# A hybrid transformer step: four accumulation groups at once after each norm, another order of work on VectorE and ScalarE, and GpSimd's low parts in half pieces

## The chip, the cores and the metric

The kernel runs on one core of one Trainium2 chip. The metric is the device time of one execution in microseconds (us), taken as the median of three runs. All arithmetic is in float32; the large matrix products run on TensorE in the fp32r form.

## The reference, cut to what matters

The reference is one inference step of a two-layer backbone with 640 tokens (512 latent and 128 context) and 1024 features. The part that matters here is the order of the norms and the projections behind them:

```python
h = rmsnorm(x, norm_g[layer, 0]) * (1 + sc1) + sh1
if layer % 2 == 0:            # layer 0: convolution module beside 4 retention heads
    u_val, u_gate, q, k, v, g = split(h @ w_in)
    y = concatenate([conv_out, ret_out]) @ w_out
else:                         # layer 1: grouped-query attention with per-head norm and rotary positions
    q, k, v = split(h @ w_qkv)
    y = blocked_attention(apply_rope(rms(q)), apply_rope(rms(k)), v) @ w_o
x = x + g1 * y
h = rmsnorm(x, norm_g[layer, 1]) * (1 + sc2) + sh2
x = x + g2 * (square(relu(h @ mlp_w1)) @ mlp_w2)
```

The scales, shifts and gates (`sh1`, `sc1`, `g1`, ...) come from a vector product `silu(cond) @ ada_w`, of which 1024x6144 weights are read per layer.

## The kernel before, in words

**Products.** The activations lie transposed in SBUF, features on the partitions, in two halves of 320 tokens. Every factor is kept as a high part and a low part (`hH`, `hL` for activations, `wH`, `wL` for weights), and a product is three matmuls per 128-feature chunk k (high by high, high by low, low by high), added up in one PSUM bank over eight chunks. `product` (L471) writes these matmuls for one or several *groups* at once; a group is one bank, that is 128 output features by 320 tokens (or 128 tokens by 256 features). Its matmul is line 479 in the profile.

**Weight tiles.** The weights come in 96 tiles of 1024x256. A tile goes through four steps, each in two halves of 1024 columns: SP loads a half into `raw`, of which there is only one copy; ScalarE rounds it into `wH` (`split`, L983); GpSimd writes `wL = raw - wH` (`lo`, L1366), and that frees the half of `raw` for the load of the next tile. `wH` and `wL` have two slots, tile t uses slot t % 2. TensorE waits for `wl_done` of the first half at chunk 0 and of the second at chunk 4 (`w_wait`).

**Pairs of tiles behind a norm.** Behind each norm stands `tile_pair` (or `qkv_pair`): two tiles, both slots, by two halves of tokens, eight groups. Groups 0 and 1 are tile 0 on the first half of tokens, 2 and 3 tile 1 on the first half, 4 and 5 tile 0 on the second half, 6 and 7 tile 1 on the second half. They run two at a time. So slot 0 is no longer read once groups 4 and 5 are done, and the `split` of the tile after the pair is put there on ScalarE.

**The norm.** DVE (VectorE) adds the squares that ScalarE makes (`square`, `add_squares`), TensorE adds them over the partitions with a product by ones (`stat`, L601), ScalarE takes the root (`std`), DVE the reciprocal (L1409, 2.2 us), and then for each chunk DVE writes `vb` (`h_value`, L1419), ScalarE `hH` (`hi`, L1004), DVE `hL` (`h_lo`, L1429). Chunk k of a half of tokens releases `h_ready`, for which TensorE waits at chunk k. The first half of tokens (`h_both`) is interleaved with the last residual updates `xT += gate * ps` (L1387) of the product before, which also free banks 0 to 3 for the pair, and with the squares of the second half. The second `stat` stands inside the first two groups of the pair.

**The heads.** The four retention heads are projected in two passes i of six tiles b. DVE does the 31 taps of the depthwise convolution in between (`taps`, L1543), cut into pieces around the heads' work. At the end ScalarE copies the last outputs to `ret`, DVE normalises them (L1618) and multiplies by the gate (L1623), TensorE turns them in 16 pieces (`turn_retention`, L610), ScalarE copies `hH`, DVE writes `hL` (L1634). Eight of these pieces stand before the output projection, eight before its chunk 7. The convolution's channel sums (L1641 to L1649) follow on DVE.

**Attention's entry.** `qkv_pair` runs keys and first queries; then come tiles 2 to 5 (`tile_n`). DVE does head norm and rotation (`rope`, L1788 to L1808), for which ScalarE takes a root (`rope_std`, L1257); TensorE turns keys and queries (`turn_keys`, L877; `turn_queries`, L889) into banks 4 to 6, and ScalarE copies them out (`turned_out`, L1264).

**The scale vectors.** `strips` (L590) multiplies 512x512 pieces of `ada_w`, which SP loads into the single buffer `ada` once the piece before is used. On SP the third piece stands behind the load of weight tile 3, because `load_ada(t)` follows `load_tile(t + 1, ...)`.

Of the kernel before, what the change touches and what calls it, by code (L numbers as in the profile page):

```python
# [71 lines left out]
N_TILES = T_MLP1 + 8 * FG  # L72

# [33 lines left out]
QKV_PAIR = ((0, 0), (0, 1), (1, 0), (1, 1), (0, 2), (0, 3), (0, 4), (1, 2), (1, 3), (1, 4))  # L107
# [66 lines left out]
def hybrid_step(nc, x_prompt, x_sample, state_ret, cache_k, cache_v, ada_w, even_w_in, even_w_out, final_g,  # L174
# [3 lines left out]
    with ctx:  # L178
# [73 lines left out]
        fr = place("fr", [P, 2, HALF])  # L252
# [48 lines left out]
        wh_done, wl_done = sem("wh_done"), sem("wl_done")  # L301
# [38 lines left out]

        block = ctx.enter_context(nc.Block())
# [3 lines left out]
        def _(sp):  # L345
# [4 lines left out]
            def load_tile(t, halves, first=False):  # L350

                for j, src in enumerate(halves):
                    if not first:
                        sp.wait_ge(wl_done, 2 * t - 1 + j)
                    n = src.shape[2]
                    sp.dma_start(raw[:, j, :].rearrange("p (k n) -> p k n", n=n), src).then_inc(raw_in[j], 16)
# [113 lines left out]
        def _(pe):  # L470
            def product(groups, nk, waits, width):  # L471


                for k in range(nk):
                    waits(k)
                    for bank, lhs, rhs in groups:
# [7 lines left out]
            def w_wait(t, k, nk):  # L484

                if k == 0:
                    pe.wait_ge(wl_done, 2 * t + 1)
                elif k == nk // 2:
                    pe.wait_ge(wl_done, 2 * t + 2)

            def tile_t(t, slot, xH, xL, free, x_wait=None, hooks=None, nk=KC, nm=2, bank0=0, inside=None, pairs=False):
# [12 lines left out]
                for n in range(0, 2 * nm, together):  # L504
# [3 lines left out]
                    def waits(k, n=n):  # L508
                        if n == 0:
                            w_wait(t, k, nk)  # L510
                        if inside and inside[:2] == (n, k):
                            inside[2]()
# [7 lines left out]
            def tile_pair(t, xH, xL, free, x_wait=None, hooks=None, nk=KC, nm=2, inside=None, together=1):  # L520
# [8 lines left out]
                for n in range(0, 4 * nm, together):  # L529
                    for q in range(n, n + together):  # L530
                        free(q)
# [8 lines left out]
                    product([group(q) for q in range(n, n + together)], nk, waits, HALF)  # L540
                    for q in range(n, n + together):
# [17 lines left out]
            def qkv_pair(t, free, x_wait, inside):  # L559
# [8 lines left out]
                for ns in ((0, 1), (2, 3), (4, 5), (6,), (7, 8), (9,)):  # L568
                    for q in ns:
                        free(q)  # L570
# [8 lines left out]
                    product([group(q) for q in ns], KC, waits, 256)  # L579
# [74 lines left out]
            for j, (n0, n1) in enumerate(((6, 9), (9, 13), (13, 16), (16, 16))):  # L654
# [4 lines left out]
                for n in range(n0, n1):  # L659
# [4 lines left out]
                      {1: [lambda: strips(0)], 5: [lambda: strips(1)]}, together=2)  # L664
# [95 lines left out]
            for n in range(8):  # L760
                turn_retention(n)

# [7 lines left out]
            for t in range(4):  # L770
                def free(n, t=t):
                    if t == 0 and n < 4:
                        pe.wait_ge(act_free, A_MLP0 - 3 + n)
                    else:
# [4 lines left out]
                       inside=(0, 7, lambda: [turn_retention(n) for n in range(8, 16)]) if t == 0 else None,  # L779
# [69 lines left out]
            def mlp(layer, norm):  # L849
# [5 lines left out]
                          inside=(0, 4, lambda: stat(norm, 1, SUMS)), together=2)  # L855
# [27 lines left out]
            def turn_queries(r):  # L883
                pe.wait_ge(ro_done, 2 * r + 4)
                pe.wait_ge(tr_out, 3 * (r + 1))
                for h in range(2):
                    cs = slice(h * P, (h + 1) * P)
                    for n, tile in enumerate(LAT_TILES):
# [7 lines left out]
                     lambda half, k: pe.wait_ge(h_ready, 16 * 2 + 8 * half + k + 1), (0, 4, lambda: stat(2, 1, SUMS)))  # L896
# [75 lines left out]
        def _(act):  # L972
# [35 lines left out]
            def before_pair_ends(norm, v0, t, start):  # L1008

                std(norm, 0)  # L1010
                hi(norm, 0, range(0, 3))
                square(norm, 12, v0, "tile")
                square(norm, 13, v0, "tile")
                split(t, 0, start - 2)
                hi(norm, 0, range(3, 6))
                square(norm, 14, v0, "tile")
                square(norm, 15, v0, "tile")
                split(t + 1, 1, start)
                hi(norm, 0, range(6, 8))
# [27 lines left out]
            hi(0, 1, range(0, 4))  # L1047
# [9 lines left out]
            hi(0, 1, range(4, 8))  # L1057
# [34 lines left out]
            for i in range(2):  # L1092
                at = 0
                for b in range(6):
# [7 lines left out]
                    for n in range(4 if b < 2 else NT):  # L1102
# [15 lines left out]
                        if b in (3, 5) and n == 3:  # L1118
                            for q in range(3):
# [5 lines left out]
                                                     ACT.Copy).then_inc(o_out, 1)  # L1125
# [821 lines left out]
```

## Time and profile before

| | |
|---|---|
| time, median of 3 runs | 1694.05 us (1691.47 to 1695.34) |
| the profiled execution's own time | 1695.47 us |
| its span, first to last instruction | 1693.7 us |
| TensorE busy | 1619.5 us, 96% |
| VectorE (DVE) busy | 770.2 us, 45% |
| ScalarE (ACT) busy | 528.1 us, 31% |
| GpSimd (POOL) busy | 503.2 us, 30% |
| mean granted TensorE clock | 0.98 |

The span is almost wholly TensorE. What a change around it is worth is read from the places where TensorE stands still. The span leaves out 1.8 us that lie around it in the execution's own time.

### The profile page before, as it was taken

The page shows a single profiled execution, that of the slowest core. Times are in us where ns is not written, and L with a number is a line of the kernel's source. Part 1 is how long each engine was busy: PE and PEld are TensorE (multiplying, and loading weights), DVE is VectorE, ACT ScalarE, POOL GpSimd, SP SyncE. Part 2 cuts the span into 40 slices and gives each one's busy share as a digit, 9 for nine tenths or more (in the row PEclk, how much of TensorE's full clock was granted, in tenths as well). Part 3 has the DMA queues.
Part 4 walks back from the last instruction along what each step waited for, and adds up shares of the span by engine and source line. Part 5 has one row for each costly group of instructions (what it writes and reads, how often), then busy time and mean ns, then how long its engine had stood idle before and what let it go on. Part 6 is the DMA issues. An engine that isn't in the chain of part 4 may idle for free.

```text
span 1693.7 us, 27621 instructions
## 1 busy us (share of the span) xinstructions
PE 1619.5 (96%) x11934; PEld 1539.0 (91%) x11934; DVE 770.2 (45%) x1438; ACT 528.1 (31%) x986; POOL 503.2 (30%) x198
## 2 busy tenths in 40 slices
PE   5899998989899999999999989999999999999998
PEld 3899998979899999999999889556999999999997
DVE  4547675656662232242232865653572241331333
ACT  3413332324442132131232423543352131231332
POOL 0335234313233333333323233000233333333331
PEclk8999999999999999999999999999999999999999
DMA  8444333202243233343343122000222222222221
GB/s 298 141 158 127 117 113 125 88 26 69 87 149 125 94 132 125 125 148 105 105 142 111 57 75 69 13 1 1 79 85 75 75 76 75 75 75 75 75 75 63
DMA packets 131019, 162.16 MB, mean 96 GB/s; under 512 B 4433, under 2 KB 103633, under 8 KB 130897
## 3 DMA queue, kind: packets, MB, share of 16 engines
q1 hardware_dynamic: 129664, 159.34, 29.0%
q8 instruction: 94, 1.54, 0.4%
q10 hardware_dynamic: 1232, 1.05, 0.2%
q14 instruction: 29, 0.23, 0.0%
HBM read 156.44 MB, written 3.93 MB: 95 GB/s over the span
## 4 chain that ended last, share of the span: by engine, by line
PE 86%; DVE 8%; ACT 2%; POOL 1%; DMA 1%; issue 1%; SPq 0%; DVEq 0%; ACTq 0%
PE ps L479 74%; PE ps L590 2%; PE ps L944 2%; DVE hL L1429 2%; POOL wL L1366 1%; PE ps L909 1%; DMA pre_over_h<-in_ada_w 1%; PE ps L685 1%; DVE amx L1819 1%; PE ps L718 1%; DVE vb L1419 1%; ACT wH L983 1%; PE ps L610 1%; PE ps L923 1%; DVE xT L1387 1%
## 5 line engine op out<-in xcount | busy, mean ns | idle before, releaser
L1366 POOL TENSOR_TENSOR wL<-raw,wH 128x1024 fp32r<-128x1024 f32 x192 | 500.2, 2626 | 1158.1 <-ACT wH L983 1157.9
L479 PE MATMUL ps<-hH,wH 128*128 128x320 f32 x1536 | 482.6, 314 | 12.5 <-DVE hL L1429 7.1
L479 PE MATMUL ps<-hL,wH 128*128 128x320 f32 x1536 | 477.3, 311 | 0.0
L479 PE MATMUL ps<-hH,wL 128*128 128x320 f32 x1536 | 477.3, 311 | 0.0
L479 PE MATMUL ps<-fH,wH 128*128 128x320 f32 x1024 | 317.6, 310 | 0.0
L479 PE MATMUL ps<-fH,wL 128*128 128x320 f32 x1024 | 316.2, 309 | 0.0
L479 PE MATMUL ps<-fL,wH 128*128 128x320 f32 x1024 | 316.2, 309 | 0.0
L479 PEld LDWEIGHTS ps<-hH,wH 128*128 128x128 f32 x1536 | 291.2, 190 | 19.4 <-issue 9.5
L983 ACT ACTIVATE wH<-raw 128x1024 fp32r<-128x1024 f32 x192 | 193.0, 1051 | 346.9 <-PE ps L479 328.9
L479 PEld LDWEIGHTS ps<-hL,wH 128*128 128x128 f32 x1536 | 291.1, 190 | 0.6 <-issue 0.4
L479 PEld LDWEIGHTS ps<-hH,wL 128*128 128x128 f32 x1536 | 290.8, 189 | 0.0
L1387 DVE SCALAR_TENSOR_TENSOR xT<-ps,modT,xT 128x320 f32<-128x320 f32 (+2 forms) x264 | 107.4, 436 | 388.3 <-PE ps L479 388.2
L1735 DVE TENSOR_TENSOR fs<-fr 128x320 f32<-128x320 f32 x128 | 79.4, 621 | 265.0 <-ACT fr L1219 264.1
L479 PEld LDWEIGHTS ps<-fH,wH 128*128 128x128 f32 x1024 | 192.5, 188 | 1.7 <-issue 1.6
L479 PEld LDWEIGHTS ps<-fL,wH 128*128 128x128 f32 x1024 | 192.5, 188 | 0.1
L479 PEld LDWEIGHTS ps<-fH,wL 128*128 128x128 f32 x1024 | 192.5, 188 | 0.0
L479 PE MATMUL ps<-wH,hH 128*128 128x256 f32 x560 | 164.6, 294 | 4.8 <-POOL wL L1366 4.3
L479 PE MATMUL ps<-wL,hH 128*128 128x256 f32 x560 | 160.2, 286 | 0.0
L479 PE MATMUL ps<-wH,hL 128*128 128x256 f32 x560 | 160.2, 286 | 0.0
L1219 ACT ACTIVATE fr<-ps 128x320 f32<-128x320 f32 x128 | 55.7, 437 | 279.3 <-PE ps L479 279.2
L479 PEld LDWEIGHTS ps<-wH,hH 128*128 128x128 f32 x560 | 109.4, 195 | 6.4 <-issue 4.0
L479 PEld LDWEIGHTS ps<-wL,hH 128*128 128x128 f32 x560 | 109.4, 195 | 0.5 <-issue 0.2
(190 smaller groups left out, 1591.5 us busy)
## 6 DMA issues: line engine op xcount, KB each, us to landing
raw<-in_mlp_w SPq DMA_DIRECT2D x128, 512.0 KB, 3.9
ada<-in_ada_w SPq DMA_DIRECT2D x40, 1024.0 KB, 5.2
raw<-in_even_w_in SPq DMA_DIRECT2D x32, 512.0 KB, 5.8
raw<-in_even_w_out SPq DMA_DIRECT2D x12, 512.0 KB, 3.6
raw<-in_odd_w_qkv SPq DMA_DIRECT2D x12, 512.0 KB, 3.6
pre_over_h<-in_ada_w SPq DMA_DIRECT2D x2, 2048.0 KB, 14.9
pre_arena<-in_ada_w SPq DMA_DIRECT2D x2, 2048.0 KB, 18.7
raw<-in_odd_w_o SPq DMA_DIRECT2D x8, 512.0 KB, 3.4
```

The lines of the kernel that those rows point to most:

```text
L479: last = nc.tensor.matmul(ps[:, bank, 0:width], a_, b_, start=(k == 0 and p_ == 0), stop=(k == nk - 1 and p_ == 2))
L590: last = nc.tensor.matmul(ps[32 * j:32 * j + 32, B_ADA, 0:P], siluc[:, 4 * part + k, :], by_lane[:, j], start=(part == 0 and k == 0), stop ...
L610: return nc.tensor.transpose(ps[:, bank, at:at + np_], src[p0:p0 + np_, tile, col0:col0 + P], ident[p0:p0 + np_, p0:p0 + np_])
L685: return nc.tensor.matmul(ps[:, bank, at:at + RV], kd_nat[:, r, tile, :], v_nat[:, tile, :], start=True, stop=True)
L718: last = nc.tensor.matmul(out, qdec[:, r, cs], S[:, r, n, :], start=False, stop=(r == 1))
L944: last = nc.tensor.matmul(ps[:, 6, :], va[:, vt, kv * P:(kv + 1) * P], pT[:, h % 2, n, :], start=(n == 0), stop=(n == 4))
L983: nc.scalar.activation(wH[:, slot, j * 1024:(j + 1) * 1024], raw[:, j, :], ACT.Copy).then_inc(wh_done, 1)
L1219: nc.scalar.activation(fr[:, n % 2, :], ps[:, n % 4, 0:HALF], ACT.Relu).then_inc(act_free, 1)
L1366: nc.gpsimd.tensor_tensor(wL[:, slot, cs], raw[:, j, :], wH[:, slot, cs].bitcast(F32), ALU.subtract).then_inc(wl_done, 1)
L1387: last = nc.vector.scalar_tensor_tensor(out=x, in0=ps[:, n % 4, c0 - half * HALF:c0 - half * HALF + w_], scalar=modT[:, gate_at + k, which ...
L1429: last = nc.vector.scalar_tensor_tensor(out=hL[:, k, c0:c0 + w_], in0=vb[:, k % 4, a_:a_ + w_], scalar=modT[:, SHIFT_AT[norm] + k, which:w ...
L1735: nc.vector.tensor_tensor(fs[:, n % 2, :], fr[:, n % 2, :], fr[:, n % 2, :], ALU.mult).then_inc(fs_done, 1)
```

## The change

- **Groups of four.** In `tile_pair` and `qkv_pair` the first four groups still run two by two, but groups 4 to 7 now run together: for each chunk twelve matmuls instead of six. In `qkv_pair` the ten groups are also renumbered, and the last two run together. ScalarE's `split` of the tile after the pair moves from behind groups 4 and 5 to behind group 7 (attention: behind group 8 of 10).
- **Later sums.** The second `stat` moves from chunk 4 to chunk 6 of the first two groups.
- **VectorE and ScalarE order around the norms.** The last residual updates and squares are interleaved earlier. In the MLP `fr` has four buffers, and ScalarE does four `relu` before the larger part of the second half's `hi`. In attention, `rope_std(0)` moves behind the `split` of tile 3, `turn_keys` from inside tile 2 to behind it, `turn_queries(0)` into tile 3, and `turned_out(0)` behind `rope_std(2)`.
- **GpSimd pieces.** Every half is written by two instructions of 512 columns instead of one of 1024.
- **VectorE low parts.** The low parts of tiles `T_HEADS + 2` and `T_HEADS + 8` move from GpSimd to DVE, behind four of the taps (`weight_lo`).
- **Heads' end.** The copies of the heads' outputs and the last root move ahead of the last two gate copies; six pieces instead of eight stand before the output projection, the other ten between its chunks; the first low part stands before the last gate product.

```diff
-                for n in range(0, 4 * nm, together):
-                    for q in range(n, n + together):
-                        free(q)
+                for ns in joint or [(n,) for n in range(4 * nm)]:
+                    n = ns[0]
+                    if len(ns) < 4:
+                        for q in ns:
+                            free(q)
...
-                      {1: [lambda: strips(0)], 5: [lambda: strips(1)]}, together=2)
+                      {1: [lambda: strips(0)], 3: [lambda: strips(1)]}, joint=((0, 1), (2, 3), (4, 5, 6, 7)))
...
-                          inside=(0, 4, lambda: stat(norm, 1, SUMS)), together=2)
+                          inside=(0, 6, lambda: stat(norm, 1, SUMS)), joint=((0, 1), (2, 3), (4, 5, 6, 7)))
...
-                for ns in ((0, 1), (2, 3), (4, 5), (6,), (7, 8), (9,)):
+                for ns in ((0, 1), (2, 3), (4, 5, 6, 7), (8, 9)):
...
-            for n in range(8):
+            for n in range(6):
                 turn_retention(n)
+            TURN_AT = {(0, 4): (6, 7), (0, 5): (8,), (0, 6): (9, 10), (0, 7): (11, 12), (2, 1): (13, 14), (2, 2): (15,)}
...
             for t in range(2, 6):
                 tile_n(T_QKV + t, t % 2, lambda n, t=t: pe.wait_ge(act_free, A_QKV + 5 * (t - 1) + n + 1), NAT_BANKS,
-                       {1: [turn_keys]} if t == 2 else None)
-                turn_queries(t - 2)
+                       {1: [lambda: turn_queries(0)]} if t == 3 else None)
+                if t == 2:
+                    turn_keys()
+                else:
+                    turn_queries(t - 2)
...
-            for n in range(2, 6):
+            hi(0, 1, range(3, 8))
+            for n in range(4, 8):
                 gate_out(n)
-            split(2, 0, G_GATE + 6)
-            gate_out(6)
-            gate_out(7)
-            split(3, 1, G_GATE + 8)
+            split(2, 0)
+            split(3, 1)
...
-                hi(norm, 1, range(4, 8))
-                hidden_hi(0, 0)
-                for n in range(2, 6):
+                hi(norm, 1, range(0, 3))
+                relu(0, 2)
+                relu(0, 3)
+                hi(norm, 1, range(3, 8))
+                for n in range(3):
+                    hidden_hi(0, n)
+                for n in range(4, 8):
                     relu(0, n)
-                split(t0 + 2, 0, g0 + 6)
-                relu(0, 6)
-                relu(0, 7)
-                split(t0 + 3, 1, g0 + 8)
+                split(t0 + 2, 0)
+                split(t0 + 3, 1)
...
-                if n == 6:
-                    split(T_QKV + 2, 0, G_QKV + 7)
+                if n == 8:
+                    split(T_QKV + 2, 0, G_QKV + 9)
+            split(T_QKV + 3, 1, G_QKV + 10)
             rope_std(0)
-            split(T_QKV + 3, 1, G_QKV + 10)
...
                     if n == 1:
                         rope_std(t - 1)
-                    if n == (3 if t == 2 else 1):
-                        turned_out(t - 2)
+                    if n == 1 and t > 2:
+                        turned_out(t - 3 if t == 3 else t - 2)
+                    if n == 3 and t == 3:
+                        turned_out(1)
...
-                    nc.gpsimd.tensor_tensor(wL[:, slot, cs], raw[:, j, :], wH[:, slot, cs].bitcast(F32),
-                                            ALU.subtract).then_inc(wl_done, 1)
+                    for c0 in (0, 512):
+                        cs = slice(j * 1024 + c0, j * 1024 + c0 + 512)
+                        last = nc.gpsimd.tensor_tensor(wL[:, slot, cs], raw[:, j, c0:c0 + 512], wH[:, slot, cs].bitcast(F32),
+                                                       ALU.subtract)
+                    last.then_inc(wl_done, 1)
...
             for t in range(N_TILES):
-                lo(t, t % 2)
+                if t not in DVE_LO:
+                    lo(t, t % 2)
...
+                    if e:
+                        taps(*cuts[0:2])
+                    else:
+                        taps(0, 4)
+                        weight_lo(T_HEADS + 6 * i + 2)
+                        taps(4, cuts[1])
...
-                       3: [lambda: wc(10)], 4: [lambda: wc(11), lambda: add_squares(1, 5, "half")],
-                       5: [lambda: wc(12)], 6: [lambda: wc(13), lambda: add_squares(1, 6, "half"), lambda: wc(14)],
+            h_both(1, {"first": [lambda: wc(8)], 0: [lambda: wc(9), lambda: wc(10)], 1: [lambda: wc(11)],
+                       2: [wc_squares(4), lambda: wc(12)], 3: [lambda: wc(13), wc_squares(5)], 4: [lambda: wc(14)],
+                       5: [lambda: wc(15)], 6: [wc_squares(6)], 7: [wc_squares(7)]})
```

## Rows read from the trace of the kernel before

**Rows 1.** TensorE's waits, whole span: line, releaser, total us, times, longest.
```profile
PE ps L601 <- DVE ssum L1405: 9.9, 3, 4.0
PE ps L479 <- DVE hL L1429: 7.6, 6, 4.1
```
**Rows 2.** Groups by line and shape: count, busy us, mean ns.
```profile
L983 ACT ACTIVATE wH<-raw 128x1024 fp32r<-128x1024 f32 x192 | 193.0, 1051 | 346.9 <-PE ps L479 328.9
L1374 POOL TENSOR_TENSOR y_nat<-y_nat,gfin 128x512 f32<-128x512 f32 x2 | 2.7, 1392 | 16.6 <-ACT y_nat L1196 16.6
L1419 DVE SCALAR_TENSOR_TENSOR vb<-xT,coef,ps 128x320 f32<-128x320 f32 x32 | 16.9, 538 | 0.0
```
**Rows 3.** The chain that ended last, two tiles: start us, us, instruction.
```profile
499.78 14.28 PE ps L479 x96
```
**Rows 4.** Timeline, TensorE after a stop at 43 us and one at 1227 us.
```profile
47.05 0.61 PE L479 MATMUL ps<-hH,wH 128*128 128x320 f32 x1 [4.11 <-DVE hL L1429]
...
51.72 0.47 PE L479 MATMUL ps<-hH,wL 128*128 128x320 f32 x1
...
1231.63 0.47 PE L479 MATMUL ps<-hL,wH 128*128 128x320 f32 x1
...
1232.70 0.47 PE L479 MATMUL ps<-hH,wL 128*128 128x320 f32 x1
```
**Rows 5.** Timeline, tile 2 and the third scale piece: start us, us, instruction.
```profile
73.94 2.00 ACT L983 ACTIVATE wH<-raw 128x1024 fp32r<-128x1024 f32 x2
75.06 4.80 POOL L1366 TENSOR_TENSOR wL<-raw,wH 128x1024 fp32r<-128x1024 f32 x2 [18.32 <-ACT wH L983]
80.30 7.69 SPq L368 DMA_DIRECT2D ada<-in_ada_w  x2
86.48 1.08 PE L590 MATMUL ps<-ada,siluc 128*32 128x128 f32 x32 [1.15 <-DMA ada<-in_ada_w]
```
**Rows 6.** Timeline, layer 0's MLP norm, TensorE, GpSimd, DVE and ScalarE.
```profile
454.16 4.91 POOL L1366 TENSOR_TENSOR wL<-raw,wH 128x1024 fp32r<-128x1024 f32 x2 [22.96 <-ACT wH L983]
454.56 2.30 DVE L1429 SCALAR_TENSOR_TENSOR hL<-vb,modT,hH 128x320 fp32r<-128x320 f32 x1
460.11 0.61 PE L479 MATMUL ps<-hH,wH 128*128 128x320 f32 x1 [5.37 <-DVE xT L1387]
470.57 0.42 PE L479 MATMUL ps<-hH,wH 128*128 128x320 f32 x1 [1.30 <-DVE hL L1429]
489.18 2.00 ACT L983 ACTIVATE wH<-raw 128x1024 fp32r<-128x1024 f32 x2
```
**Rows 7.** Timeline, tile `T_HEADS + 8`: GpSimd, TensorE, DVE.
```profile
244.82 19.68 POOL L1366 TENSOR_TENSOR wL<-raw,wH 128x1024 fp32r<-128x1024 f32 x2 [8.76 <-ACT wH L983]
262.19 0.36 PE L479 MATMUL ps<-wH,hH 128*128 128x256 f32 x1 [3.57 <-POOL wL L1366]
271.46 0.69 DVE L1571 SCALAR_TENSOR_TENSOR prob<-ps,dmat 128x512 f32<-128x512 f32 x1 [9.20 <-PE ps L679]
```
**Rows 8.** Timeline, heads' end, TensorE.
```profile
356.04 3.70 PE L610 MATMUL ps<-const,ret 128*128 128x128 f32 x12 [3.33 <-DVE hL L1634]
380.59 1.12 PE L766 MATMUL ps<-cst,ones 128*128 128x512 f32 x2 [0.63 <-DVE cst L1649]
```
**Rows 9.** Timeline, attention's entry, all engines.
```profile
951.28 1.41 PE L601 MATMUL ps<-ssum,ones 128*128 128x320 f32 x2 [3.05 <-DVE ssum L1405]
981.40 0.29 ACT L1257 ACTIVATE rss<-rss,eps 128x10 f32<-128x10 f32 x1
983.50 2.91 DVE L1804 TENSOR_TENSOR kro<-rn,tabs 128x640 f32<-128x640 f32 x1
992.31 1.11 PE L877 MATMUL ps<-const,kro 128*128 128x128 f32 x4 [5.47 <-DVE kro L1808]
```
**Rows 10.** Timeline, layer 1's MLP norm, TensorE and DVE.
```profile
1230.16 1.41 PE L601 MATMUL ps<-ssum,ones 128*128 128x320 f32 x2 [2.89 <-DVE ssum L1405]
1235.12 2.15 DVE L1409 RECIPROCAL ps<-rstd 128x320 f32<-128x320 f32 x1
```

More of the change, by code:

```diff
@@ L72 @@
 N_TILES = T_MLP1 + 8 * FG
+DVE_LO = (T_HEADS + 2, T_HEADS + 8)
 G_X = 0
@@ L470, in _, with product @@
         def _(pe):
-            def product(groups, nk, waits, width):
+            def product(groups, nk, waits, width, free=None):
                 for k in range(nk):
                     waits(k)
-                    for bank, lhs, rhs in groups:
+                    for n, (bank, lhs, rhs) in enumerate(groups):
+                        if free and k == 0:
+                            free[n]()
                         (aH, aL), (bH, bL) = lhs(k), rhs(k)
@@ L539, in waits @@
                             x_wait(n // (2 * nm), n // nm % 2, k)
-                    product([group(q) for q in range(n, n + together)], nk, waits, HALF)
-                    for q in range(n, n + together):
+                    product([group(q) for q in ns], nk, waits, HALF, [lambda q=q: free(q) for q in ns] if len(ns) == 4 else None)
+                    for q in ns:
                         for hook in (hooks or {}).get(q, ()):
@@ L578, in waits @@
                             x_wait(n // 4, k)
-                    product([group(q) for q in ns], KC, waits, 256)
+                    product([group(q) for q in ns], KC, waits, 256, [lambda q=q: free(q) for q in ns] if len(ns) == 4 else None)
             def strips(p):
@@ L778, in _ @@
                        {0: {2: [lambda: channel_stat(0)]}, 1: {2: [lambda: channel_stat(1)]}}.get(t),
-                       inside=(0, 7, lambda: [turn_retention(n) for n in range(8, 16)]) if t == 0 else None,
+                       inside=lambda n, k: [turn_retention(q) for q in TURN_AT.get((n, k), ())] if t == 0 else None,
                        pairs=(t == 0))
@@ L1010, in before_pair_ends @@
                 std(norm, 0)
-                hi(norm, 0, range(0, 3))
                 square(norm, 12, v0, "tile")
+                hi(norm, 0, (0,))
                 square(norm, 13, v0, "tile")
+                hi(norm, 0, (1,))
                 split(t, 0, start - 2)
-                hi(norm, 0, range(3, 6))
+                hi(norm, 0, (2, 3))
                 square(norm, 14, v0, "tile")
+                hi(norm, 0, (4,))
+                split(t + 1, 1, start)
+                hi(norm, 0, (5,))
                 square(norm, 15, v0, "tile")
-                split(t + 1, 1, start)
-                hi(norm, 0, range(6, 8))
+                hi(norm, 0, (6, 7))
                 std(norm, 1)
@@ L1442, in h_both @@
             def h_both(norm, later):
+                for step in later.get("first", ()):
+                    step()
                 reciprocal_std(norm, 0)
@@ L1703, in squares @@
                     return lambda: add_squares(norm, first // 2 + q, "tile")
[L1705 to L1706 removed]
+                h_both(norm, {0: [lambda: update(first + 4)], 1: [lambda: update(first + 5)], 3: [squares(2)],
+                              4: [lambda: update(first + 6)], 6: [lambda: update(first + 7)], 7: [squares(3)]})
             def wc(n):
```

107 lines of the change are left out of this document (61 added, 46 removed).

## The prediction

> **What bounds the kernel now.** I read the engines' busy times first: TensorE works for 96% of the span, so only its stops can be won. Its waits come next [rows 1]: the sums behind a norm cost 9.9 us in three stops, the low parts `hL` 7.6 us. The timeline then gives each place that the change touches: 5.37 us before layer 0's MLP and 1.30 us inside its first groups [rows 6]; 3.57 us for a weight tile's low part [rows 7]; 3.33 and 0.63 us at the heads' end [rows 8]; 3.05 and 5.47 us at attention's entry [rows 9]; 2.89 us before layer 1's MLP [rows 10]; 4.11 us at the start [rows 4]. Behind a stop TensorE runs on at the lower of its two levels, 1.2 instead of 2.4 GHz: matmuls start 0.27 us apart instead of 0.149 us [rows 3, 4]. After the stop before 47.05 this lasts 18 matmuls (the first and the last are shown), 0.12 us each, 2.2 us; after 1230 us about 7, 0.8 us. I charge 1.6 us for each stop of 3 us or more, from between these ends.
>
> **The price of a tile that isn't prepared.** A half tile costs ScalarE 1.05 us [rows 2] and GpSimd half of 4.80 us, 2.4 us [rows 5]. For two pieces of 512 columns the bounds are 2.4 us (cut with no loss) and 2.7 us, from the nearest row, a GpSimd product of 512 columns at 1.39 us, two in 2.7 us [rows 2]. I take 2.5 us, near the like work. By the Trainium skill ("GPSIMD Engine Reference", dispatch) a two-input instruction pays about 2.5 cycles for each element and some tens of cycles at its start; at its clock that is an estimated 1.1 us for a piece, and each of the four entries below would be 0.3 us cheaper. With 0.2 us of handing over, TensorE waits 1.05 + 2.5 + 0.2 = 3.75 us from the moment ScalarE starts `split`.
>
> **Groups of four.** Now slot 0 is refilled while groups 6 and 7 run: in the MLP pair that ends near 495 us, ScalarE starts at 489.18 us [rows 6], and no wait follows. When groups 4 to 7 share the chunks, tile 0 is read until the pair ends, and `split` stands behind ScalarE's whole work on group 7. No tile is ready: a new stop at all four pairs. Queued behind this `split` are the next one, the relus and, through the single `raw`, the next loads.
>
> *Gate pair.* The pair ended near 81.8 us (86.48 less 1.15 and one group of 24 matmuls, 3.6 us). The first `hL` is freed by a shorter GpSimd piece, 0.9 us earlier, so it now ends at T = 80.9. The sigmoid copies take 0.5 us, so tile 2 enters at T + 4.3. Worse, the third scale piece is loaded behind both halves of tile 3, so behind GpSimd's second half, T + 6.8. Before, the transfer was issued 0.4 us behind that half and TensorE resumed 6.2 us after the issue [rows 5]. That gives 94.3 us instead of 86.48: 7.8 us, and a clock tail: **+9.4 us** (5.0 if the transfer were hidden).
>
> *MLP, layer 0.* TensorE waited at 460.11 for the update of residual 13, and its last chunk started at 470.57. I replayed the new DVE order with the instructions' own times: an operation on 320 columns takes 0.54 us [rows 2], in a row 0.46 us from start to start; so `h_value` and `h_lo` 0.46 each, a residual (two operations) 0.59, a pair of sums 0.93, the reciprocal 2.15 us [rows 10]. All of it is 17.5 us from 443, plus an estimated 2.5 us lost to GpSimd. Residual 13 is done at 451, before TensorE leaves the product in front, and the last `hL` comes near 463. Groups 0 and 1 end at 464.0 instead of 471.45: -7.45. At the pair's end four relus and three `hidden_hi` keep ScalarE for 1.9 us more, so the entry is 1.9 + 3.75 = 5.65 us, and a tail of 1.6: together **-0.2 us**. The late `hi` of the second half costs nothing: with twelve matmuls a chunk, 1.76 us, against 1.17 us for DVE, it is covered.
>
> *MLP, layer 1.* By the same replay the last `hL` comes at 1231.0 instead of 1235.1 [rows 10], and groups 0 and 1 end 3.6 us earlier. The entry and its tail are 7.2: **+3.6 us**.
>
> *Attention.* The same order brings groups 0 and 1 3.2 us forward, and the rest of the pair 1.0: -4.2. Moving `turn_keys` behind tile 2 takes away 5.5 us and its tail: -6.9. The entry of tile 2 costs a copy more, 4.2 + 1.6 = +5.8. And `rope_std(0)`, at 981.40 before [rows 9], now stands behind the `split` of tile 3, whose `raw` can only be loaded once tile 2's low parts are done (983); for half the bytes of the scale piece, which took 6.2 us, I take 4 us: the root comes near 988. The keys are rotated by 997, TensorE comes to `turn_queries(0)` at 1005.9, but that needs `turned_out(0)`, which on ScalarE stands behind `rope_std(2)`, which needs the second rotation and the third's sum of squares, 11.9 us of DVE work, on which GpSimd's pieces can lie (a 0.8 us product took 2.91 us beside them [rows 9]). Between 1009 and 1013, then 2 us of root and copies: a stop of 5.7 to 10 us, I take 7.9 and a tail. Sum **+4.2 us** (2.0 to 6.5).
>
> **Low parts on DVE.** For `T_HEADS + 8` GpSimd needed 19.68 us beside the taps [rows 7], which hold the inputs it needs. On DVE it costs 2.3 us, hidden: DVE waited 9.20 us for this head's scores [rows 7]. The stop of 3.57 us and its tail go: **-5.2 us**.
>
> **Heads' end.** The low part of piece 0 goes ahead of the gate product, so piece 4 no longer waits 3.33 us; piece 5 waits 0.9 us behind that product. TensorE would reach the channel sums 4.6 us earlier, but DVE's sums, for which it already waits 0.63 us [rows 8], run beside GpSimd and follow only 2 to 4 us earlier. Between -1.9 and -4.6, I take **-3.6 us**.
>
> **GpSimd pieces.** A DVE `hL` started 0.4 us behind a GpSimd half took 2.30 instead of 0.55 us, until that half was over [rows 6]. Pieces halve the longest block, and double the times that GpSimd must get in; I have put this in above. The Trainium skill says so too ("SBUF — State Buffer", two separate sides): the pair of ports goes to whoever starts first, for the whole instruction. By that rule alone the total blocked time stays, as I have counted it.
>
> **Sum.** 9.4 - 0.2 + 3.6 + 4.2 - 5.2 - 3.6 = +8.2 us on a span of 1693.7, 1701.9; with 1.8 around it 1703.7 against the profiled 1695.47. That execution is 1.4 above the median, so 1694.05 + 8.2 = 1702.3 us.
>
> **Rivals.** (a) *The pieces take the port wait away*, faster: DVE slips in between pieces and never loses time. Then groups 0 and 1 never wait for `hL`: -1.7 (gate), -2.35, -2.5, -1.3 at the other norms, rotation -2.2, channel sums -0.8, GpSimd at its cheap end -1.0: -11.85, so -3.7, 1690.4 us. For: the block ends exactly with GpSimd's instruction [rows 6]. Against: the total work of both on the port is the same. It must save over 11.6 us to come out faster. (b) *GpSimd starves*: cut in pieces, another tile beside the taps is late, and the stop of 262.19 comes back [rows 7]: +5.2, 1707.5 us. Against: right behind 262 DVE was free for 9.20 us. (c) *The clock stays high* over the five new stops: -8.0, 1694.3 us, no change. Against: stops of 2.9 and 4.1 us both brought the lower level [rows 4].
>
> **How the numbers follow.** My forecast has 0.65, (a) 0.15, (b) 0.10, (c) 0.10. A measurement tells 0.2% (3.4 us) from no change. The bounds of the terms give my forecast 1696 to 1710. To hold 8 in 10 the range reaches to most of (a): 1691.5 to 1710.5. Slower: 0.57 of my case and (b), and part of (c): 0.70. Same: 0.16. Faster: most of (a), 0.14.
>
> **What the profile would show.** Four stops of TensorE behind the pairs, of about 4.3, 5.7, 4.2 and 5.7 us, released by GpSimd's `wL`, and one by the scale piece near 90 to 94 us; a stop of `turn_queries(0)` released by ScalarE's `kTa`; no stop at 460, 951, 992, 1230 and 262 us; a wait of L601 at most small. I would be wrong if the entries cost under 3 us, if the scale piece is there by then, or if the first groups still wait for residuals.

## The result and the profile after

The changed kernel takes 1732.19 us (median of 4 runs, 1729.88 to 1735.1); the kernel before, run beside it, 1694.69 (1691.47 to 1695.43). The ratio is 1.0224, 95% interval 1.0209 to 1.0239: 37.5 us slower. The forecast was 1702.3 us with a range up to 1710.5, so the direction was right and the size was missed by nearly four fifths (8.2 of 37.5 us).

The profiled execution has a span of 1731.0 us against 1693.7. The head of its page (span; busy time by engine) and, of TensorE's waits, those that the change touches (line waiting, releaser: sum, times, longest) are these:

```profile
span 1731.0 us, 27785 instructions
PE 1625.7 (94%) x11934; PEld 1546.4 (89%) x11934; DVE 735.7 (42%) x1442; ACT 534.3 (31%) x989; POOL 513.8 (30%) x382
```

```profile
PE ps L489 <- POOL wL L1394: 21.0, 5, 5.8
PE ps L489 <- DVE hL L1459: 19.6, 5, 5.4
PE ps L904 <- ACT kTa L1293: 9.7, 1, 9.7
PE ps L603 <- DMA ada<-in_ada_w: 4.9, 2, 4.0
PE ps L614 <- DVE ssum L1435: 4.5, 3, 3.9
PE ps L603 <- DVE adaT L1515: 4.1, 2, 2.1
PE ps L781 <- DVE cst L1699: 3.1, 1, 3.1
```

These answer to [rows 1]. The sums behind a norm cost 4.5 instead of 9.9 us, as the change intends, and 3.94 of that stands in front of the gate pair, as before. But the waits for `hL` rose from 7.6 to 19.6 us, and those for a weight tile's low part, `wL`, are now the largest. The mean granted clock is 0.974 against 0.980: by that share of the two spans an estimated 11 of the 37 us are slow clock. Next, from the timeline of TensorE: start, length, operation, and in brackets the stop ahead of it with its releaser.

```profile
86.28 0.58 PE L489 MATMUL ps<-hH,wH 128*128 128x320 f32 x1 [4.13 <-POOL wL L1394]
95.57 1.08 PE L603 MATMUL ps<-ada,siluc 128*32 128x128 f32 x32 [3.98 <-DMA ada<-in_ada_w]
276.18 1.08 PE L603 MATMUL ps<-ada,siluc 128*32 128x128 f32 x32 [2.04 <-DVE adaT L1515]
363.25 0.96 PE L623 MATMUL ps<-const,ret 128*128 128x128 f32 x3 [1.00 <-DVE hL L1572]
389.79 0.95 PE L781 MATMUL ps<-cst,ones 128*128 128x512 f32 x1 [3.06 <-DVE cst L1699]
475.27 0.51 PE L489 MATMUL ps<-hH,wH 128*128 128x320 f32 x1 [4.84 <-DVE hL L1459]
509.96 0.61 PE L489 MATMUL ps<-hH,wH 128*128 128x320 f32 x1 [5.83 <-POOL wL L1394]
969.34 0.58 PE L489 MATMUL ps<-wH,hH 128*128 128x256 f32 x1 [4.66 <-DVE hL L1459]
1001.88 0.55 PE L489 MATMUL ps<-wH,hH 128*128 128x256 f32 x1 [4.15 <-POOL wL L1394]
1035.92 1.09 PE L904 MATMUL ps<-const,qro 128*128 128x128 f32 x4 [9.70 <-ACT kTa L1293]
1258.94 0.63 PE L489 MATMUL ps<-hH,wH 128*128 128x320 f32 x1 [5.39 <-DVE hL L1459]
1291.85 0.61 PE L489 MATMUL ps<-hH,wH 128*128 128x320 f32 x1 [5.84 <-POOL wL L1394]
```

The four stops behind the pairs stand at 86.28, 509.96, 1001.88 and 1291.85 us. Three stops of 4.7 to 5.4 us at the norms are in no part of the forecast. Placing the same matmuls (a strip, the sums of a norm, the first scores, the last turned tiles) side by side in both traces gives a ledger:

| stretch, up to | before | after | change | forecast |
|---|---|---|---|---|
| strip behind the gate pair | 101.77 | 112.38 | +10.6 | +9.4 |
| heads and their end, to the first sums of norm 1 | 441.82 | 452.63 | +0.2 | -8.8 |
| MLP 0, to those of norm 2 | 932.62 | 948.95 | +5.5 | -0.2 |
| q, k, v, to the first scores | 1054.93 | 1081.69 | +10.4 | +4.2 |
| attention, to those of norm 3 | 1211.48 | 1237.01 | -1.2 | 0 |
| MLP 1, to the last turned tiles | 1684.17 | 1721.56 | +11.9 | +3.6 |
| sum | | | +37.4 | +8.2 |

What holds the norm in front of MLP 0 is seen on the other engines (same columns):

```profile
462.44 6.13 POOL L1394 TENSOR_TENSOR wL<-raw,wH 128x512 fp32r<-128x512 f32 x4 [19.90 <-ACT wH L1001]
466.42 0.53 DVE L1449 SCALAR_TENSOR_TENSOR vb<-xT,coef,ps 128x320 f32<-128x320 f32 x1
469.42 1.06 ACT L1001 ACTIVATE wH<-raw 128x1024 fp32r<-128x1024 f32 x1 [3.02 <-DMA raw<-in_mlp_w]
472.47 1.06 ACT L1001 ACTIVATE wH<-raw 128x1024 fp32r<-128x1024 f32 x1 [1.99 <-DMA raw<-in_mlp_w]
473.43 0.55 ACT L1022 ACTIVATE hH<-vb,modT 128x320 fp32r<-128x320 f32 x1
474.01 1.21 DVE L1459 SCALAR_TENSOR_TENSOR hL<-vb,modT,hH 128x320 fp32r<-128x320 f32 x1 [4.10 <-ACT hH L1022]
```

GpSimd frees the second half of the one `raw` tile only at 468.57 us. ScalarE's next `split` waits 3.02 and 1.99 us for the loads that follow. The changed order puts `hi` of chunk 5 behind this `split`, where the kernel before has it in front: it runs at 473.43 us, though its input, the `vb` at 466.42, was ready by 466.95. Until then VectorE stands 4.10 us, and TensorE 4.84. In front of MLP 1 it is the same, with ScalarE waiting 2.00 and 3.36 us.

### The profile page after: what moved, and what is told of

The parts are those of the page before. It is cut to its first block, busy times and chain, and to the rows that moved or that the text cites. A ratio compares the mean times of both kernels' runs of the same rounds, so it can differ in the third digit from the quotient of the medians.

```text
span 1731.0 us, 27785 instructions
## 1 busy us (share of the span) xinstructions
PE 1625.7 (94%) x11934; PEld 1546.4 (89%) x11934; DVE 735.7 (42%) x1442; ACT 534.3 (31%) x989; POOL 513.8 (30%) x382
## 4 chain that ended last, share of the span: by engine, by line
PE 84%; DVE 8%; DMA 3%; POOL 2%; ACT 2%; issue 1%; SPq 0%; DVEq 0%; ACTq 0%
PE ps L489 73%; PE ps L603 2%; PE ps L962 2%; POOL wL L1394 2%; DVE cacc L1590 2%; PE ps L927 1%; DMA pre_over_h<-in_ada_w 1%; PE ps L698 1%; DMA ada<-in_ada_w 1%; DVE amx L1871 1%; ACT wH L1001 1%; PE ps L731 1%; PE ps L623 1%; PE ps L941 1%; DMA raw<-in_mlp_w 1%
## 5 line engine op out<-in xcount | busy, mean ns | idle before, releaser
L1394 POOL TENSOR_TENSOR wL<-raw,wH 128x512 fp32r<-128x512 f32 x376 | 510.9, 1389 | 1185.1 <-ACT wH L1001 1185.1
L489 PE MATMUL ps<-hH,wH 128*128 128x320 f32 x1536 | 487.3, 317 | 31.7 <-POOL wL L1394 16.8
L489 PEld LDWEIGHTS ps<-hL,wH 128*128 128x128 f32 x1536 | 294.6, 192 | 0.4 <-issue 0.2
L1787 DVE TENSOR_TENSOR fs<-fr 128x320 f32<-128x320 f32 x128 | 74.4, 583 | 300.7 <-ACT fr L1244 299.6
```

The lines of the kernel that those rows point to most:

```text
L489: last = nc.tensor.matmul(ps[:, bank, 0:width], a_, b_, start=(k == 0 and p_ == 0), stop=(k == nk - 1 and p_ == 2))
L1394: last = nc.gpsimd.tensor_tensor(wL[:, slot, cs], raw[:, j, c0:c0 + 512], wH[:, slot, cs].bitcast(F32), ALU.subtract)
L1787: nc.vector.tensor_tensor(fs[:, n % 2, :], fr[:, n % 4, :], fr[:, n % 4, :], ALU.mult).then_inc(fs_done, 1)
```

## The experiments

All compute the whole of the reference's work. Each is compared with the kernel before on the same chip. The kernel before took 1691.37 us (median) on the chip of the three runs that start from all three moves, and 1695.02 to 1695.48 on the others, so a difference in us between two versions from different chips can be off by up to 4 us; where it matters, the ratios decide. The first four start from the changed kernel.

**Second split behind chunk 5.** In all three norms:

```diff
-                split(t + 1, 1, start)
                 hi(norm, 0, (5,))
                 square(norm, 15, v0, "tile")
+                split(t + 1, 1, start)
                 hi(norm, 0, (6, 7))
```

> The changed kernel with one entry of ScalarE's queue moved in each of three norms (before MLP 0, before the q, k, v projections, before MLP 1): the second weight tile's split goes behind the sixth chunk's high part and the last squares, where the kernel before has it. Theory (queue order): in the changed kernel the high part of chunk 5 stands in ScalarE's queue behind a split that waits for its raw tile (ScalarE idle 3.02 + 1.99, 1.56 + 2.26 and 2.00 + 3.36 us on the DMA), and TensorE stops 4.84, 4.66 and 5.39 us for that chunk. Moved, the three stops go to under 1.5 us each and the time falls by 9 to 15 us, to 1717 to 1723. Rival (the weights are late anyway, because the GpSimd pieces and the port hold the raw buffers): the stop moves to the next group, which waits for the second tile's low part, and the time falls by less than 3 us.

Measured 1728.87 us, ratio 1.0200 (1.0176 to 1.0225): 3.3 us less than the changed kernel, whose interval (1.0209 to 1.0239) overlaps this one. The expected 9 to 15 us didn't come. ScalarE and TensorE of this run show why:

```profile
471.77 1.06 ACT L1001 ACTIVATE wH<-raw 128x1024 fp32r<-128x1024 f32 x1 [0.99 <-DMA raw<-in_mlp_w]
472.74 1.00 ACT L1022 ACTIVATE hH<-vb,modT 128x320 fp32r<-128x320 f32 x2
474.98 0.63 PE L489 MATMUL ps<-hH,wH 128*128 128x320 f32 x1 [3.23 <-DVE hL L1459]
```

The split now delays chunks 6 and 7 instead: the three stops are 3.23, 3.48 and 2.57 us, and all are still for `hL`. The size agrees with the rival, the mechanism doesn't, since it had the stops move to `wL`. So this run didn't settle it.

**The keys' root ahead of the second split** behind the q, k, v pair:

```diff
-            split(T_QKV + 3, 1, G_QKV + 10)
             rope_std(0)
+            split(T_QKV + 3, 1, G_QKV + 10)
```

> The changed kernel with two neighbours of ScalarE's queue swapped behind the q, k, v pair: the root of the keys' norm goes ahead of the split of the pair's second successor tile, where the kernel before has it. Theory: the root was ready to run when VectorE's sums ended at 1000.9 and ran at 1008.66, behind a split that waited 5.41 + 1.26 us for its raw tile; VectorE then idled 8.07 us, its chain over the keys and the first queries ran late, and the 9.70 us stop at turn_queries(0) is its end. Swapped, that stop falls by 5 to 8 us, and the time to 1724 to 1727. Rival (the stop is set by ScalarE's queue further on, by the root of the second queries at 1034.02, or by VectorE operations drawn out by GpSimd, 1.9 us instead of 0.82): less than 2 us.

Measured 1727.28 us, 1.0184 (1.0160 to 1.0208). The 9.70 us stop is 2.22 us here: the theory's stop, at the edge of its time. Part of the gain went to a new stop of 1.30 us at 1005.85, for the second half of a low part `wL`: beside VectorE's operations, which now come earlier, GpSimd's four pieces took 7.21 instead of 5.38 us.

**Whole halves on GpSimd.** Each half is again written by one instruction of 1024 columns:

> The changed kernel with GpSimd's low parts as one instruction per half of 1024 columns again. Theory A (the pieces cost next to nothing: a pair of pieces takes 2.48 us where the kernel before shows 2.36 to 2.4 for a half, and lets VectorE in between): the time falls by 0 to 3 us or rises by up to 2. Rival B (the pieces are what makes the low parts late, 6.13 us for four pieces beside VectorE in front of MLP 0 where the kernel before shows 4.91 for two halves, and their delay is passed on by the raw buffers): the entry stops of 4.84, 4.66 and 5.39 us shrink by a third or more, and the time falls by 5 us or more.

Measured 1729.39 us, 1.0213 (1.0181 to 1.0245). The time is theory A's: 2.8 us, less than these intervals tell apart. Of the three stops at the norms, 4.59, 2.02 and 4.06 us here, only the second shrank by a third, and behind it the sums wait 2.12 us.

**Groups of two.** The second halves of all four pairs run two by two again. With this go ScalarE's old order of copies, high parts and splits, the old numbering of the q, k, v groups, and the second strip back behind group 5. Two places of the edit:

```diff
-                          inside=(0, 6, lambda: stat(norm, 1, SUMS)), joint=((0, 1), (2, 3), (4, 5, 6, 7)))
+                          inside=(0, 6, lambda: stat(norm, 1, SUMS)), joint=((0, 1), (2, 3), (4, 5), (6, 7)))
...
-                for n in range(4, 8):
-                    relu(0, n)
-                split(t0 + 2, 0)
-                split(t0 + 3, 1)
+                for n in range(2, 6):
+                    relu(0, n)
+                split(t0 + 2, 0, g0 + 6)
+                relu(0, 6)
+                relu(0, 7)
+                split(t0 + 3, 1, g0 + 8)
```

> The changed kernel with the second halves of the four tile pairs in groups of two again, together with ScalarE's order of copies, high parts and splits that goes with it (gate, MLP 0, MLP 1, and the q, k, v pair with its old order of groups); the norms' order, the later sums, the GpSimd pieces, the heads and the order of keys and queries stay as changed. Theory (groups of four free the two weight slots only at the pair's end): the four stops behind the pairs (4.13, 5.83, 4.15, 5.84 us, all for the second tile's low part) and the one for the third strip (3.98) go, with the slow-clock stretches behind them; what groups of four save at the pairs' entries comes back. The time falls by 17 to 27 us, to 1705 to 1715. Rival (the splits only move the wait: the port and the raw tiles bound it anyway): under 8 us.

Measured 1698.79 us, 1.0020 (1.0007 to 1.0034): 33.4 us less, more than the 17 to 27 expected. All four stops behind the pairs are gone, and the third strip waits 1.31 us instead of 3.98. Nothing came back at the entries: with groups of two the first stop inside the gate pair is 0.36 us, with groups of four 0.33.

**Groups of four alone,** on the kernel before, with the order of copies and splits and the second strip behind group 3, which tests the same from the other side:

> The kernel before with groups of four at the four pairs and the order of copies and splits that goes with them, and nothing else of the change. Theory (the groups of four carry the loss wherever they stand): four stops behind the pairs of 4 to 6 us for the second tile's low part, one of 3 to 4 us for the third strip, and the slow clock behind them: 25 to 34 us slower than before, 1720 to 1729. Rival (as the prediction had it: at the entries groups of four give much of that back, because chunks are wanted at half the pace): 8 to 18 us slower, 1703 to 1713.

Measured 1723.82 us, 1.0179 (1.0160 to 1.0199): 28.8 us slower, as the theory has it. Its waits for a low part `wL` sum to 23.9 us. Its stops inside the gate pair and the one of MLP 0, near the entry:

```profile
59.22 0.42 PE L481 MATMUL ps<-hH,wH 128*128 128x320 f32 x1 [1.40 <-DVE hL L1434]
482.28 0.42 PE L481 MATMUL ps<-hH,wH 128*128 128x320 f32 x1 [0.97 <-DVE hL L1434]
```

They stand almost as in the kernel before (1.43 and 1.30 us). Both fall inside groups 0 and 1, which the change leaves joined as they were. Behind them the kernel before has no stop inside these two pairs, so that asking for the second half's chunks at half the pace had nothing to win.

**Split last,** on the version with groups of two: `split(t + 1, 1, start)` behind `hi(norm, 0, (6, 7))` in all three norms.

> The run with groups of two (1698.79 us), and in the three norms the second weight tile's split moved behind all eight high parts instead of behind the fifth. Theory (queue order; the run that moved it behind chunk 5 alone only moved the stop to chunk 6, which then stood behind it): the entry stops of 4.66, 4.49 and 3.85 + 0.77 us go to 1.5 us or less each. The following group waits for its low parts or the half's root for up to 2 us each, so that 4 to 10 us are gained: 1689 to 1695. Rival (VectorE's own chain, drawn out by GpSimd, is what is late): 2 us or less, 1697 or more.

Measured 1681.95 us, 0.9920 (0.9891 to 0.9949): 16.8 us less, more than the 4 to 10 expected. The stops are now for low parts `wL` and short: 0.85, 2.06 and 1.65 us. The windows show the rest (stretch and length; busy us and instructions of PE, PEld, DVE, ACT and POOL; granted clock, DMA share, GB/s); the first three rows are the version with groups of two, the next three this one:

```profile
462.00:480.00 18.00, 17.75 (x155) 16.12 (x156) 16.72 (x42) 8.58 (x24) 1.29 (x1) 0.91 0.48 152
948.00:960.00 12.00, 11.07 (x70) 10.34 (x71) 11.08 (x24) 4.65 (x14) 1.65 (x2) 0.76 0.27 86
1232.00:1245.00 13.00, 11.52 (x56) 10.72 (x57) 12.08 (x27) 5.48 (x15) 1.80 (x2) 0.74 0.25 77
```

```profile
460.00:480.00 20.00, 19.04 (x175) 17.54 (x174) 16.95 (x45) 11.25 (x27) 5.01 (x4) 1.00 0.52 174
940.00:960.00 20.00, 17.83 (x139) 16.71 (x138) 17.55 (x48) 11.59 (x28) 5.00 (x4) 1.00 0.30 93
1222.00:1240.00 18.00, 16.35 (x111) 15.96 (x110) 15.23 (x42) 11.00 (x27) 5.01 (x4) 1.00 0.20 59
```

A clock of 0.91 over 18 us, 0.76 over 12 and 0.74 over 13 is up to 1.6, 2.9 and 3.4 us of work lost (the share of the clock missing, by the time). With the short stops the clock stays at 1.00. The two profiled spans differ by 13.6 us (1697.2 and 1683.6).

**Nine taps first,** on the version with groups of two. In the changed kernel VectorE stands in front of the weight tile's low part with taps left to do, and its row of modulations comes late:

```profile
140.96 2.36 DVE L1565 TENSOR_TENSOR wL<-raw,wH 128x1024 fp32r<-128x1024 f32 x2 [5.90 <-ACT wH L1001]
159.25 0.32 DVE L1515 STREAM_TRANSPOSE adaT<-ps 128x128 f32<-128x128 f32 x1
159.72 0.53 PE L603 MATMUL ps<-ada,siluc 128*32 128x128 f32 x12 [2.05 <-DVE adaT L1515]
```

```diff
-                            taps(0, 4)
+                            taps(0, 9)
                             weight_lo(T_HEADS + 6 * i + 2)
-                            taps(4, cuts[1])
+                            taps(9, cuts[1])
```

> The run with groups of two (1698.79 us), and in the heads VectorE's low parts of the first head's value tile after nine filter taps instead of after four. Theory (VectorE stands 5.90 and 4.49 us in front of the split it needs with taps left to do, so its row of modulations comes late and TensorE stops 2.05 and 2.04 us at the strips behind): both stops go, with any slow clock behind them, and the time falls by 4 to 6 us, to 1693 to 1695. Rival (the stops come from the low parts' own 4.6 us on VectorE, wherever they stand): no change beyond 1 us.

Measured 1695.46 us, 1.0003 (0.9993 to 1.0014): 3.3 us less. Both stops are gone, and the size is a little under the range.

**All three moves,** on the version with groups of two:

> The run with groups of two and all three moves of order: split last in the norms, nine taps ahead of the low parts, and the root of the keys' norm ahead of the second split behind the q, k, v pair. Theory: the gains add, 4 to 10, 4 to 6 and 5 to 7 us off 1698.79, 1676 to 1686, faster than both kernels. Rival (what is taken off one stop comes back at the next stage, since VectorE's chain and the raw tiles pace each entry): 1690 or more.

Measured 1679.09 us, 0.9914 (0.9899 to 0.9929), faster than both kernels. But that is only 2.9 us under split last, a difference within the intervals, and the taps alone had given 3.3; so no gain of the earlier root can be seen here. `turn_queries(0)` still stops 8.53 us instead of 9.26, for the copies of the turned keys.

**Keys copied first,** on that version:

```diff
+                    if n == 1 and t == 3:
+                        turned_out(0)
                     if n == 1:
                         rope_std(t - 1)
-                    if n == 1 and t > 2:
-                        turned_out(t - 3 if t == 3 else t - 2)
+                    if n == 1 and t > 3:
+                        turned_out(t - 2)
```

> The run with all three moves of order (1679.09 us), and at the third of the q, k, v tiles ScalarE's copies of the turned keys ahead of the root of the second queries' norm. Theory (queue order again): the keys were turned by 979.3, the copies ran at 991.93, behind a root that waited 6.20 us for VectorE's sums, and TensorE stopped 8.53 us in turn_queries(0); the first queries were ready at 988.7. Moved, the stop ends at the queries, 3 to 4 us long, and the time falls by 4 to 7 us, to 1672 to 1675. Rival (VectorE is what paces this stretch; its next chain starts no earlier, so the stop turns up at the next turning): 1677 or more.

Measured 1670.79 us, 0.9869 (0.9846 to 0.9893). The stop before the edit and after it:

```profile
991.72 0.30 ACT L1282 ACTIVATE rss<-rss,eps 128x10 f32<-128x10 f32 x1 [6.20 <-DVE rss L1842]
991.93 1.07 ACT L1289 ACTIVATE kTa<-ps 128x512 f32<-128x512 f32 x2
993.63 1.08 PE L904 MATMUL ps<-const,qro 128*128 128x128 f32 x4 [8.53 <-ACT kTa L1292]
```

```profile
989.11 0.65 PE L904 MATMUL ps<-const,qro 128*128 128x128 f32 x4 [3.73 <-DVE qro L1862]
```

The stop ends at the rotated queries now, as the theory said. The gain is 8.3 us by the times and 7.6 by the ratios, since this version ran on another chip than the one it starts from; both are above the 4 to 7 expected. This is the fastest version run, 1.3% under the kernel before.

**The old order of keys and queries,** on the version with all three moves:

> The run with all three moves of order (1679.09 us), and the order of turned keys and queries as in the kernel before (keys inside the second tile, each turning right behind its tile, ScalarE's copies to match). Theory: the stop of 8.53 us in turn_queries(0) goes and the kernel before's stop for the keys, 5.47 us, comes back, smaller because the entry is no longer late or larger by what the port costs: the time changes by -5 to +1 us, 1674 to 1680. Rival (turning the keys later was a gain, as the prediction booked it with 6.9 us): 1683 or more.

Measured 1675.42 us, 0.9899 (0.9876 to 0.9922). The stop for the keys is back at 5.44 us in place of the 8.53 us. By the times this is 3.7 us better than all three moves, and 4.6 us worse than the version with the keys copied first, on the same chip. Its interval overlaps those of both, so that turning the keys later pays only together with copying them first is likely but not shown.

**Whole halves again,** on the version with all three moves:

> The run with all three moves of order (1679.09 us), and GpSimd's low parts as one instruction per half. Theory (pieces cost 0.1 us per half and 376 of them, yet almost none of it on the path; beside VectorE in front of a norm they cost or gain 1 to 2 us a place): within 3 us of 1679, either side. Rival A (the pieces' loss, 2.8 us in the changed kernel, stays): 1674 to 1677. Rival B (the pieces let VectorE in and so carry part of the gain at the entries): 1682 or more.

Measured 1684.64 us, 0.9953 (0.9934 to 0.9971): rival B, 5.6 us slower without the pieces (6.6 by the ratios). TensorE's first stops inside the gate pair and the one of MLP 0:

```profile
58.35 0.54 PE L489 MATMUL ps<-hH,wH 128*128 128x320 f32 x1 [1.43 <-DVE hL L1457]
457.73 0.41 PE L489 MATMUL ps<-hH,wH 128*128 128x320 f32 x1 [0.64 <-DVE hL L1457]
```

The gate pair's stop of the kernel before is back. The two traces differ by 7.3 us (spans of 1676.8 and 1684.1), and 3.7 of it are there at the third strip (85.58 us with pieces, 89.31 without). But not all of that is the stop. The kernel before has the same stop, and yet a higher clock than this run; first this run's window, then that of the kernel before:

```profile
40.00:90.00 50.00, 42.28 (x371) 39.67 (x374) 27.57 (x55) 22.49 (x42) 18.35 (x8) 0.85 0.39 127
```

```profile
40.00:90.00 50.00, 43.31 (x394) 41.21 (x394) 27.30 (x55) 22.54 (x42) 19.17 (x8) 0.91 0.41 131
```

The 0.06 between them is up to 3.0 us over 50. So what the pieces are worth depends on the clock behind a stop of 1.4 us, which one profile doesn't fix.

**Pieces alone,** on the kernel before:

> The kernel before with GpSimd's low parts in pieces of 512 columns and nothing else of the change. Theory (what the run with whole halves showed, 5.6 us lost in the reordered kernel, is VectorE let in between the pieces at the norms): the stops at the entries of the four pairs (1.43, 1.30 + 5.38, 3.05 + 0.33, 2.89 + 0.30 us) lose 1 to 2 us a place, and the time falls by 2 to 6 us, 0.1 to 0.35%. Rival (as the prediction booked it, and as the changed kernel lost 2.8 us by the pieces: the low parts come later and nothing else moves): unchanged or up to 3 us slower, 0 to 0.2%.

Measured 1693.58 us, 0.9992 (0.9981 to 1.0003), 1.7 us less, with an interval that holds both no change and the theory's smallest gain. The sums' stops shrink as the theory says, but the next chunk stops instead:

```profile
947.68 0.78 PE L601 MATMUL ps<-ssum,ones 128*128 128x320 f32 x2 [1.07 <-DVE ssum L1407]
953.10 0.39 PE L479 MATMUL ps<-wH,hH 128*128 128x256 f32 x1 [3.22 <-DVE hL L1431]
```

## Why the prediction was wrong

The forecast's own terms split in two. The groups of four (9.4 at the gate pair, 7.25, 5.8 and 7.2 at the other three) make 29.7 us; 28.8 and 33.4 were measured. The rest of the change was to win 21.5 us; as it was ordered it lost 3.3. So the step that failed is the replay of the norms' order, and after it the terms of the heads (-8.8 in all, where the ledger has +0.2).

- **Groups of four.** The mechanism was right and sized well: stops of 4.13, 5.83, 4.15 and 5.84 us against 4.3, 5.65, 4.2 and 5.65, `split` at 82.53 and TensorE at 86.28, 3.75 us as worked out. The strip resumed at 95.57 against 94.3. The pair itself ended at 82.15, not at 80.9: the shorter pieces took the stop inside it from 1.43 to 0.33 us, but the second strip, asked for earlier, waits 0.95 us for its load. The clock behind the pair was under-sized: 0.83 over 86 to 96 us and 0.90 over 96 to 113, 0.17 by 10 and 0.10 by 17, 3.4 us, against one tail of 1.6:

```profile
86.00:96.00 10.00, 5.73 (x40) 5.50 (x44) 0.49 (x1) 2.12 (x2) 7.05 (x7) 0.83 0.62 210
96.00:113.00 17.00, 17.00 (x144) 16.61 (x140) 2.10 (x6) 2.01 (x2) 3.43 (x4) 0.90 0.38 125
```

- **The norms.** The terms -7.45, -4.2 and -3.6 failed; this is the main error. Where the forecast had the pairs end that much earlier, they ended 1.7 us earlier in MLP 0 (504.13 less 495.05 is 9.1, against +10.8 ahead of it), and by the same sum about 0.4 later in q, k, v and 3.2 later in MLP 1. The step was "I replayed the new DVE order with the instructions' own times": the replay had VectorE's queue and an allowance for GpSimd, and took ScalarE's `hi` as always on time. But the second `split` had moved ahead of `hi` of chunk 5, and the `raw` tile that it waits for lands after GpSimd's low part of the tile in front. The two runs with moved splits show it: with the split behind chunk 5 the stop moves one chunk on; with the split behind all chunks it goes, and 16.8 us with it. That this one order was the cause is shown for the version with groups of two; with groups of four it wasn't tried. "The first groups still wait" was named among what would make the forecast wrong, but for residuals, and no rival carried it.
- **Attention.** The chain of `rope_std(0)`, `rope_std(2)` and `kTa` was right, stop and releaser, 9.70 us being at the end of its range of 5.7 to 10. The stretch missed by 6.2 us: 4.6 of it are the norm's. The run with the root first took 7.5 us off this stop.
- **Low parts on DVE.** "It costs 2.3 us, hidden" failed. It priced `T_HEADS + 8` by the time that VectorE had idle later on, and `T_HEADS + 2` not at all. Both low parts stand among the taps, and in front of them VectorE stood 4.49 and 5.90 us for the split, with taps left to do. The stop of 3.57 us [rows 7] went; two of 2.05 and 2.04 came, and the -5.2 was -1.7 (the +0.2 of that stretch less the +1.9 below). The run with nine taps took both away.
- **Heads' end.** "Follow only 2 to 4 us earlier" was too kind. The stop of 3.33 us became 1.00, and the one for the channel sums rose from 0.63 to 3.06: both are released by VectorE. Together with a stretch of slow clock (TensorE 1.6 us further back by the second product of the sums, 403.15 against 392.33) the forecast -3.6 was +1.9. No run takes this part of the change by itself.
- **Pieces.** The 2.5 us for two pieces was right (2.48 us, so 1.24 for one, above the estimate of 1.1). Their effect was taken as none by itself: on the kernel before that holds within the interval, in the version with all three moves they are worth 5.6 us, part of it slow clock. By the Trainium skill ("SBUF — State Buffer", two separate sides) whoever starts first keeps the ports for the whole instruction; the trace agrees: in the three later norms the longest single `hL` takes 1.21 us, where behind the start of a whole half it took 2.30 [rows 6].
- **The rivals.** (a) had the first groups never wait for `hL`; they waited 4.84, 4.66 and 5.39 us for it, behind ScalarE's queue. (b) didn't come: no stop for a low part stands in the heads. (c) was wrong: the clock behind the other three pairs fell to 0.88 over 509 to 525 us and to 0.76 over 1001 to 1015 and 1291 to 1305, up to 1.9, 3.4 and 3.4 us, against 1.6 each. The forecast's clock terms sum to 5.0 us (8.0 for five stops, less 3.0 for two that go), where the profiles show about 11.

Summed, groups of four are 33.4 of the 37.5 us (28.8 on the kernel before); the rest of the change, as it was ordered, cost 3.3; in a better order on ScalarE and VectorE, and with groups of two, it gains about 20 (1670.79 against 1691.37 on the same chip).

What stays open: why the granted clock falls behind some stops of 1.4 to 2 us and not behind others; whether split last would do as much with groups of four; and what the later sums and the new heads' end do alone. The 28.8 and 33.4 us differ by 4.6. The traces place 3.6 of it at one stop: in the kernel before, the wait for the rotated keys fell from 5.47 to 1.90 us with groups of four, whose stop now stands ahead of it, while in the changed order the wait at `turn_queries(0)` is 9.26 us with groups of two and 9.70 with groups of four.

## What to carry to other kernels

When a chain is replayed over a new order, replay every engine that hands a link over, with its whole queue: an entry that waits for a transfer is priced by what stands behind it, not by its own length. By the Trainium skill ("PSUM — Partial Sum Buffer", engine vs sequencer instructions) the queues of ScalarE, VectorE and GpSimd are strictly first in, first out; the trace agrees, and moved entries of such queues were worth 3.3 (taps), 4.9 (root), 8.3 (copies of the keys) and 16.8 us (split last) here. And reusing loaded chunks in larger groups keeps the weight slots longer: count what the slots' next tenants cost at the group's end before counting what the group saves.

## What the runs showed of the hardware

Removing waits gave more than their length where the lower clock went too: 9.6 us of stops at the norms went (14.2 to 4.6), and the profiled clocks of 0.91, 0.76 and 0.74 went to 1.00; the gain was 16.8 us. The stop of 2.04 us for `adaT` shows how much the code doesn't set. In the changed kernel it is followed by a clock of 0.88 over 14 us, in the version with groups of two by 1.00, and in split last by 0.89, though the last two run the same code up to there. Their rows in this order:

```profile
276.00:290.00 14.00, 13.82 (x126) 13.65 (x127) 11.33 (x17) 2.83 (x7) 4.75 (x4) 0.88 0.47 152
```

```profile
265.00:280.00 15.00, 14.73 (x147) 14.57 (x148) 12.84 (x17) 3.07 (x8) 4.88 (x4) 1.00 0.43 141
```

```profile
265.00:280.00 15.00, 14.70 (x133) 14.53 (x134) 12.04 (x17) 2.83 (x7) 4.89 (x4) 0.89 0.44 141
```

So a single profile can show or hide 0.11 by 15, 1.7 us, that no edit made.
